# Output projection of a hybrid attention and mixture-of-experts block: the last two parts produced by contraction steps, and one pair of transposes moved ahead

## The reference, cut to what matters

```python
x = x + concat([sb, pool]) @ w_out            # output projection and residual
h2 = rms_norm(x, norm2_g)
logits = h2 @ w_router + b_router             # 32 experts
top_val, top_idx = top_k(logits, 4); gates = softmax(top_val)
x = x + sum over chosen experts of gate * (((up + 1) * g * sigmoid(1.702 * g)) @ w_down)
return rms_norm(x, final_norm_g)
```

## Time and profile before

| | us |
|---|---|
| median of 3 runs | 1028.99 |
| lowest and highest | 1026.61, 1030.57 |
| the profiled execution, its own time | 1026.54 |
| its span, first to last instruction | 1024.7 |
| TensorE busy in it | 978.2 (95%) |
| data moved | 418.51 MB, mean 408 GB/s |

### The profile page before, as it was taken

How to read it: one execution, slowest core, us unless ns; L and a number is a source line. 1 busy time by engine, 2 the same in 40 slices (tenths; PEclk the granted TensorE clock), 3 DMA queues, 4 the chain that set the end, 5 groups by cost and what they waited for, 6 DMA issues and landing times.

```text
span 1024.7 us, 10998 instructions
## 1 busy us (share of the span) xinstructions
PE 978.2 (95%) x4612; PEld 417.5 (41%) x4612; DVE 215.0 (21%) x472; ACT 109.0 (11%) x185; POOL 8.5 (1%) x27
## 2 busy tenths in 40 slices
PE   9999999999999999999999999999999989899997
PEld 7685544343434333333434343432434333333432
DVE  2244423111121110121211112110212112121112
ACT  4252200000000000000000000000000000000102
POOL 0011000000000000000000000000000000000000
PEclk9999999999999999999999999999999999999999
DMA  9967799999999999999999999999999999999995
GB/s 343 419 259 294 265 381 427 405 436 430 430 430 430 429 430 431 437 422 427 429 421 431 438 430 430 431 430 429 429 430 433 431 430 430 432 430 427 436 421 214
DMA packets 27212, 418.51 MB, mean 408 GB/s; under 512 B 2970, under 2 KB 3890, under 8 KB 9012
## 3 DMA queue, kind: packets, MB, share of 16 engines
q1 hardware_dynamic: 25664, 417.08, 96.2%
q10 hardware_dynamic: 1524, 1.08, 0.4%
HBM read 417.10 MB, written 1.05 MB: 408 GB/s over the span
## 4 chain that ended last, share of the span: by engine, by line
PE 72%; DMA 22%; DVE 3%; issue 2%; ACT 1%; SPq 0%; DVEq 0%; ACTq 0%
PE bank L1424 58%; DMA ring<-in_w_gate_up_dram 15%; PE acc L1424 12%; DMA ring<-in_w_down_dram 7%; PE bank L1836 1%; DVE area L1234 1%; DVE area L1231 1%; ACT wpool L817 1%; DVE area L1170 0%; DMA late<-in_x_dram 0%; PE bank L1454 0%; DVE sel L930 0%; DVE area L1238 0%; ACT late L891 0%; PE bank L1655 0%
## 5 line engine op out<-in xcount | busy, mean ns | idle before, releaser
L1424 PE MATMUL bank<-ring,area 128*64 128x512 f32 (+1 forms) x1832 | 413.5, 597 | 13.1 <-DMA ring<-in_w_gate_up_dram 13.1
L1424 PEld LDWEIGHTS bank<-ring,area 128*64 128x64 f32 (+1 forms) x1832 | 133.7, 139 | 284.0 <-issue 259.4
L1424 PE MATMUL bank<-ring,wpool 128*64 128x512 f32 x864 | 192.3, 596 | 9.7 <-ACT wpool L817 5.2
L1228 DVE TENSOR_SCALAR area<-bank 128x512 f32<-128x512 f32 x31 | 21.4, 691 | 445.9 <-PE bank L1424 445.9
L1424 PEld LDWEIGHTS bank<-ring,wpool 128*64 128x64 f32 x864 | 60.1, 137 | 121.8 <-issue 110.8
L813 ACT ACTIVATE bank<-area 128x512 f32<-128x512 f32 x32 | 19.2, 602 | 496.8 <-DVE area L1228 496.8
L1424 PE MATMUL bank<-masks,xres 128*128 128x128 f32 x492 | 62.9, 281 | 2.1 <-DVE masks L1147 0.3
L1424 PEld LDWEIGHTS bank<-masks,xres 128*128 128x128 f32 x492 | 57.3, 191 | 17.7 <-issue 16.6
L1252 DVE COPY wide<-bank 64x512 f32<-64x512 f32 x30 | 20.8, 694 | 199.1 <-PE bank L1424 192.8
L1424 PE MATMUL acc<-wide,masks 128*128 128x512 f32 x120 | 55.5, 605 | 0.0
L1424 PE MATMUL bank<-area 128*64 128x512 f32 (+2 forms) x228 | 46.8, 559 | 0.5 <-DVE area L1003 0.5
(11 more groups left out here) (198 smaller groups left out, 433.7 us busy)
## 6 DMA issues: line engine op xcount, KB each, us to landing
ring<-in_w_gate_up_dram SPq DMA_DIRECT2D x50, 4096.0 KB, 26.9
ring<-in_w_down_dram SPq DMA_DIRECT2D x54, 2048.0 KB, 25.3
ring<-in_w_gate_up_dram SPq DMA_DIRECT2D x13, 2048.0 KB, 13.2
area<-in_w_gate_up_dram SPq DMA_DIRECT2D x5, 4096.0 KB, 23.3
late<-in_w_down_dram SPq DMA_DIRECT2D x5, 2048.0 KB, 17.7
area<-in_w_gate_up_dram SPq DMA_DIRECT2D x3, 2048.0 KB, 11.1
ring<-in_w_down_dram SPq DMA_DIRECT2D x6, 1024.0 KB, 38.3
ring<-in_w_in_dram SPq DMA_DIRECT2D x8, 512.0 KB, 9.0
```

Source lines behind the costliest of these rows:

```text
L1228: v.tensor_scalar(gatec, gbank[:], LIMIT, None, ALU.min).then_inc(gc, 1)
L1424: return t.matmul(o, l, r, start=start, stop=stop, skip_group_check=True)
```

## The change

Parts 3 and 4 take their 256 columns as two whole contraction steps: the moving operand is `w_o[:, k, HALF:D]` read through `by_steps`, steps s and s + 1, that is two rows of 128 elements with 16 bytes between elements. Their banks then hold step order, and `residual(3)` and `residual(4)` add them as plain 256 contiguous columns. Part 3 gives steps 4 and 5, part 4 steps 6 and 7. The transposes of steps 4 and 5 move ahead of `logits((0, 1))` and of the wait for `tr_a`, behind a new wait for `x2_ok` 4; those of steps 6 and 7 stay behind `x2_ok` 5.

```diff
+        STEPPED = OUT_PARTS[3:]
...
             def residual(n):
                 tt, b, lo, w = OUT_PARTS[n]
                 dve.wait_ge(wo_ok, max(1, n))
-                rows = step_cols(tt, lo, w)
-                v.tensor_tensor(rows, rows, by_steps(bank[b][:, 0:w]), ALU.add).then_inc(x2_ok, 1)
+                rows, more = step_cols(tt, lo, w), by_steps(bank[b][:, 0:w])
+                if OUT_PARTS[n] in STEPPED:
+                    rows, more = xres[:, tt, lo:lo + w], bank[b][:, 0:w]
+                v.tensor_tensor(rows, rows, more, ALU.add).then_inc(x2_ok, 1)
...
-                for tt, b, lo, w in OUT_PARTS[n:n + parts]:
-                    m = mm(bank[b][:, 0:w], mixT[r][:, tt * P:(tt + 1) * P], w_o[:, k, lo:lo + w],
+                for part_of in OUT_PARTS[n:n + parts]:
+                    tt, b, lo, w = part_of
+                    cols = w_o[:, k, lo:lo + w]
+                    if part_of in STEPPED:
+                        s = (lo - HALF) // P
+                        cols = by_steps(w_o[:, k, HALF:D])[:, s:s + 2, :]
+                    m = mm(bank[b][:, 0:w], mixT[r][:, tt * P:(tt + 1) * P], cols,
                            start=(k == 0), stop=(k == KD - 1))
...
             output(4, 7, 1).then_inc(wo_ok, 1)
+            pe.wait_ge(x2_ok, 4)
+            turn_last(4, 4, 2)
             pe.wait_ge(tr_a, 9)
             logits((0, 1))
             pe.wait_ge(x2_ok, 5)
-            turn_last(4, 4, 2)
             turn_last(5, 6, 2)
             logits((2, 3))
```

## The result

| | before | after |
|---|---|---|
| median of 6 runs, us | 1028.86 | 1036.29 |
| lowest and highest | 1026.25, 1031.87 | 1033.94, 1037.79 |
| span of the profiled execution | 1024.7 | 1033.1 |

The ratio is 1.0073 with a 95% interval of 1.0056 to 1.0089: the changed kernel is slower by about 7.4 us (5.8 to 9.2), 0.7%. Ratios and intervals stand here as they were recorded with the runs; they are not the quotients of the two medians and can differ from them by about a tenth of a per cent. No change was forecast (1029.4, range 1025.8 to 1032.4). The rival that came true was given 0.16, and 0.05 for the part of it that counts as slower.

The account below looks back on a forecast made before the run. The weight stream was taken to bound the expert loop, its start set by TensorE's front. -0.22 and -0.12 for the reordering, 0 for residuals and +0.7 for scattered reads gave +0.4 us on 1028.99: 1029.4, range 1025.8 to 1032.4.

Parts of the forecast that it names:

- The rival that came true: Scattered read paces the 32 passes of parts 3 and 4: 4.1 us more, 1033.1; chance 0.16, 0.05 beyond 0.17 a pass.
- What bounds the kernel: Expert loop ends with the weight stream; TensorE time won or lost before the load at 122.20 moves the end equally.
- The transposes moved ahead: Between part 4's passes and the logits: transposes of steps 4 and 5 fill TensorE's wait, a gain of 0.34 us.
- both terms: Transposes fill TensorE's wait for ScalarE after part 4, -0.22 us; VectorE's first copy starts earlier for the logits, -0.12 us.
- The 0.06 us to spare: Before the last two transposes: residual(4) still sets their time, with 0.06 us margin over the logits passes.
- The residuals: Adding parts 3 and 4 on VectorE with plain 256-column reads changes nothing: 0.42 us either way.
- The moving operand read across: 32 passes of parts 3 and 4 with 16 bytes between elements: 0 to 4.4 us, taken as 0.7.
- upper end: Price of the 32 passes from weight loads' own durations, 209 against 140 ns: 0.138 us a pass, 4.4 us.
- point of decision: Passes of parts 3 and 4 count as slower from 0.17 us added to each, 0.39 instead of 0.218.
- The nearest row: Experts' transposes at L1836, stationary operand read at 16 bytes: 0.120 us against 0.109 contiguous, source of the 0.7 us.
- the slow case: Passes of parts 3 and 4 paced by the scattered read, each element in another 16-byte line: 1033.1; chance 0.16.
- The sum: Whole change: -0.22 - 0.12 + 0.7 = +0.4 us, giving 1029.4.

Follow-up runs that it names:

- the doses: Against the kernel before: parts 3 and 4 by pairs, only part 4 at step 4, both, then part 2 too; end moved -0.3, 2.8, 7.4, 15.1 us.
- experiment 6: TensorE alone, without the kernel's work: transposes and short matmuls at different steps; transposes took 0.109 to 0.120 us, ordinary float32 stationary operand at step 4 0.233.
- experiment 1: TensorE alone, without the kernel's work: 32 float32 or 64 bfloat16 matmuls a line, one feature changed each; float32 step 1 0.216 us a pass, step 4 0.451.

## Why the prediction was wrong

**What bounds the kernel: right in what the sum needed.** A shift of TensorE's front reaches the end, in full within the runs' scatter, as the doses show. That the experts' stretch is then paced by the stream and not by TensorE's own work is argued from the windows (DMA share 1.00, TensorE idle for 32 us of 650) and not shown by the doses: either would pass on the shift. One row was also read loosely: from 124 to 150 us the stream moved 378 GB/s, and only from 150 us on 427 to 429. Nothing in the sum hangs on it.

**The transposes moved ahead: right, both terms.** -0.22 and -0.12 were forecast, 2.73 to 2.39 us was measured, and undoing the move alone brought the 2.73 back. All four signs named for it (two transposes directly behind part 4, the copies apart, the first right behind residual(4), 2.39 us) stand in the trace. The 0.06 us to spare held: the second pair advances the chain by 0.28, its own 0.22 and 0.06 of waiting.

**The residuals: right.** The operation of residual(4) takes 0.42 in both kernels.

**The moving operand read across: this step failed.** It was put at 0.022 us a pass and 0.7 in all, with an upper end of 0.138 and 4.4. Measured are 0.235 and 7.5, ten times the value taken and well past the end that was to bound it: four passes in 1.81 us, where 0.96 was forecast and even the rival named 1.4. The mechanism of the rival was right, and its point of decision (0.17 us a pass) was passed. Two errors lie in it:

- The price was carried over from a transpose's stationary operand. "The nearest row" was near by its 16 bytes only. It was another operand, and experiment 6 shows that this load alone, of all float32 forms tried in SBUF, doesn't pay per line: five groups of 32 transposes with different steps lie within 0.011 us of each other.
- The upper end was made from the same row, so it wasn't an upper end for anything else. The text itself noted that a pass needs a column every 0.85 ns. An honest bound would have asked what a source twice as slow would give, 32 x 0.218 = 7.0 us, since no row excluded it; the measured 7.5 lies close to that. The rule of the Trainium skill (Advanced Engine Details and Errata, section SBUF Cachelines) on lines of 16 bytes stood beside the sum, spoke for the slow case, and was set aside because a row of another kind seemed to disagree. The case got a chance of 0.16, too little when no row showed a moving operand at this step.

**The sum.** With the measured price it is -0.22 - 0.12 + 7.52 = +7.2 us, on the 1028.86 of these runs 1036.0; measured 1036.29.

## What to carry to other kernels

Count the 16-byte lines that a matmul's moving operand reads, each return to a line anew: in these runs each cost TensorE 1.76 ns. A float32 pass nearly keeps its pace at one line for two elements (0.227 against 0.216 us) and doubles at one line for each; a bfloat16 pass has already doubled at one line for two. If columns have to be gathered out of a row, gather neighbours in pairs and undo the order where the result is read or written; both VectorE's view across a bank and a write across PSUM were free here. A price read off one operand or one mode of an engine is no bound for another: when the trace has no row of the same kind, let the range take in a halved rate.

## What the runs showed of the hardware that was not expected

- A pass is paced by the larger of lines and columns: 1.76 ns for a 16-byte line of the moving operand, in float32 (steps 3, 4 and 8: 0.340, 0.451, 0.460 us for 256 columns) and in bfloat16 (steps 4 and 8: 0.227, 0.452). A line that the read comes back to later is paid again: two rows in the same 128 lines and four rows in the same 64 both take 0.451.
- The price of a line did not follow TensorE's clock. At a granted clock of 0.50 (L124 of experiment 1) a pass with 256 lines took 0.452 us, against 0.451 at 1.00.
- An ordinary float32 stationary operand pays as well: 0.233 us for 128 columns at step 4. The pace is the same 0.233 for passes of 256 and of 128 columns, so it is the load that sets it: 1.82 ns an element.
- A transpose's stationary operand doesn't pay (0.109 to 0.120 us at steps 1 to 8), and a bfloat16 one at 16 bytes hardly (0.056 to 0.061).
- Writing PSUM in a scattered order left the pace at 0.216 us for 256 columns and 0.429 for 512.
